# A hybrid encoder layer whose expert weights stream through a ring: the ring's slabs, the order of the loads and their size are changed

## The chip, the cores and the metric

The kernel runs on one core of one Trainium2 chip. The metric is the device time of one execution in microseconds (us). Before the change it is 1153.33 us, the median of three runs (1152.59 to 1154.02).

## The reference

One layer of an encoder over 256 tokens of width 1024: latent attention beside a convolution module, cross-attention into 256 memory tokens, and a mixture of experts; then a last RMSNorm. All in fp32. The part that matters here is the mixture (cut):

```
logits = t @ w_router + b_router              # 256 tokens, 32 experts
top_val, top_idx = lax.top_k(logits, 4)
gates = softmax(top_val)
# for the tokens of each expert e:
up = xb @ w_up[e] + b_up[e]                   # w_up[e]: 1024 x 2048, 8 MB
glu, lin = min(up[:, :1024], 7), clip(up[:, 1024:], -7, 7)
act = glu * sigmoid(1.702 * glu) * (lin + 1)
y = act @ w_down[e] + b_down[e]               # w_down[e]: 1024 x 1024, 4 MB
out = sum over the experts of a token of gate * y
return rmsnorm(x + out, g_final)
```

Each of the 32 experts has 12 MB of weights (12.58 million bytes), 402.7 million bytes in all, and every one is used once.

## The kernel before

A trunk (both mixing layers, cross-attention, router) runs first, to about 241 us. Then TensorE goes through the experts 0 to 31 in order. The tokens of an expert are taken in blocks of 64; an expert with more than 64 tokens takes a second round over the same weights (`Fori(0, extra + 1)` in `expert`), so there may be more blocks than experts. One block on PE is: the up products in four quarters (L1813), the combine of the block before (L1773), transposes of the up result (L1866), the one-hots of the combine (L1909, L1911), the gather for the next block (L1760), the first half of the down products (L1858), the columns of the next block (L1767), the second half of the down products (L1858).

**The ring.** `ring` is 20 slabs of 8 KB in each of the 128 partitions (1 MB a slab). Two slabs are a group, also called a slot: 10 slots. An expert is six groups: up 0 to 3 (the quarters of the up products) and down 4 and 5 (the halves). Here (e, i) stands for group i of expert e. Group i of expert e lies in slot (6e + i) modulo 10 (`slot_of`). During the trunk the ring holds the trunk's weights and temporaries.

**The queue of loads.** All weight loads are issued by SP, in program order, on one queue of the 16 DMA engines. Before each load SP waits until PE has finished with what lies in its slots: `up_steps` counts PE's used up quarters, `down_steps` its used down halves, and `last_block(e)` reads from a table which block is the last one of expert e. An SP wait holds back every load behind it.

- Experts 2, 3 and 28 to 31: loads of one group (2 MB, 16 KB in a row per partition), L446 and L450.
- Experts 4 to 27 (`load_expert_wide`): three loads of two groups each (4 MB, 32 KB in a row per partition). The first two, L511, bring up 0 and 1, then up 2 and 3; the third, L523, the down weights. Their waits are:

```
sp.wait_ge(up_steps, n2 * UPS + UPS)        # n2: last block of e - 2
load_wide(up_v, e, j * LOADS, 0)
sp.wait_ge(down_steps, n2 * DOWNS + DOWNS)
load_wide(up_v, e, j * LOADS, 2)
sp.wait_ge(up_steps, n1 * UPS + DOWNS)      # n1: last block of e - 1
```

PE waits for the semaphore of a load before the first group in it.

**Loops.** SP and PE have the experts 0 to 6 written out, 7 to 26 in a loop of four turns of five experts (10 slots and 6 groups repeat after five experts), and the last five written out. DVE, ACT and GpSimd loop over the experts.

**Around the first expert.** Before the table of blocks is known, SP loads expert 0 whole and the up weights of expert 1 (all 20 slabs) and `g_final` (L473, into half of `buf_v`). The down weights of expert 1 follow in four loads of one slab (L489), as PE frees the first four slabs; for that, expert 0's first two quarters are computed in halves (`first_up_half`).

**The last expert** is taken in smaller pieces, so that little is left after its last load. Its output, scaled by `g_final`, goes through `buf_x` to HBM.

## Time and profile before

| | before |
|---|---|
| median of three runs | 1153.33 us |
| the profiled execution | 1153.83 us |
| its span in the trace | 1152.1 us |
| around the span | 1.73 us |
| PE busy | 1130.9 us (98%) |
| bytes read from HBM | 436.18 MB, 379 GB/s over the span |

The profile page gives for each engine its busy time, then the span in 40 slices with the granted clock of TensorE and the rate of the DMA engines, then the chain of work that ended last. TensorE's clock was granted at full speed (1.00) in all but a few slices late in the expert stage (0.91 from 920 to 940 and from 980 to 1000 us). A busy share of PE near 1 tells little alone: it also has to be seen where PE waits for a load, and whether the DMA engines pause. "To landing" is the time from the issue of a load on SP to the semaphore that tells of its end; a load that stands in the queue behind others takes longer to land than it takes to move.

### The profile page before, as it was taken

To read this page: it belongs to the slowest core of one execution; us is meant where nothing else is said; L and a number is where in the kernel's file an instruction comes from. 1 tells how busy PE (TensorE), PEld (TensorE's weight loads), DVE (VectorE), ACT (ScalarE), POOL (GpSimd) and SP (SyncE) were. 2 spreads that over 40 slices of the span, in tenths; PEclk is the share of its full clock that TensorE was granted. 3 is DMA by queue.
4 is the path that set the end of the run, shared out by engine and by line. 5 is a ranking of instruction groups with operands and counts; after the bars stand their busy time and mean duration, and the time that the engine had idled before them with its cause. 6 is when DMAs were issued, how large, how long until landed. Compare 5 with 4: busy or idle time off the path is not lost.

```text
span 1152.1 us, 16029 instructions
## 1 busy us (share of the span) xinstructions
PE 1130.9 (98%) x5376; PEld 502.2 (44%) x5377; DVE 358.9 (31%) x933; ACT 221.7 (19%) x429; POOL 85.2 (7%) x206
## 2 busy tenths in 40 slices
PE   9999999999999999999999999999999999999999
PEld 6785487653333333333333333333333333333333
DVE  6898413232222222222222222222222222222223
ACT  5321213121111121111111111111111111111113
POOL 2990000000000000000000000000000000000000
PEclk9999999999999999999999999999999999999999
DMA  9464336389999999999999999999999999999995
GB/s 364 188 272 176 146 146 282 156 347 429 429 435 431 427 433 433 427 432 433 396 421 437 437 422 433 437 432 423 437 437 424 431 437 433 424 426 429 424 426 244
DMA packets 28821, 437.76 MB, mean 380 GB/s; under 512 B 4017, under 2 KB 4657, under 8 KB 12017
## 3 DMA queue, kind: packets, MB, share of 16 engines
q1 hardware_dynamic: 27920, 436.10, 89.4%
q10 hardware_dynamic: 864, 1.14, 0.3%
q8 instruction: 27, 0.44, 0.2%
q14 instruction: 10, 0.07, 0.0%
HBM read 436.18 MB, written 1.05 MB: 379 GB/s over the span
## 4 chain that ended last, share of the span: by engine, by line
PE 77%; DMA 20%; SPq 1%; ACT 1%; issue 0%; DVE 0%; ACTq 0%; DVEq 0%
PE bank L1813 28%; DMA ring<-in_w_up_dram 20%; PE bank L1858 16%; PE total L1773 4%; PE bank L1760 4%; PE bank L1452 2%; PE bank L1471 2%; PE bank L1866 2%; PE bank L1683 2%; PE bank L1462 2%; PE bank L1767 1%; PE bank L1617 1%; PE total L1617 1%; DMA ring<-in_w_in_dram 1%; PE bank L1911 1%; PE bank L1576 1%
## 5 line engine op out<-in xcount | busy, mean ns | idle before, releaser
L1813 PE MATMUL bank<-ring,buf_m 128*64 128x512 f32 (+1 forms) x2192 | 465.2, 581 | 13.4 <-DMA ring<-in_w_up_dram 13.3
L1813 PEld LDWEIGHTS bank<-ring,buf_m 128*64 128x64 f32 x2192 | 156.9, 138 | 316.1 <-issue 286.4
L1858 PE MATMUL bank<-ring,buf_m 128*64 128x512 f32 x1056 | 239.9, 595 | 0.0
L1343 DVE COPY buf_f<-bank 128x512 f32<-128x512 f32 x32 | 22.1, 692 | 448.6 <-PE bank L1813 448.6
L1858 PEld LDWEIGHTS bank<-ring,buf_m 128*64 128x64 f32 x1056 | 72.8, 136 | 136.5 <-issue 126.5
L888 ACT ACTIVATE buf_m<-buf_f 128x256 f32<-128x256 f32 x32 | 13.3, 416 | 333.1 <-DVE buf_f L1353 333.1
L1773 PE MATMUL total<-buf_m,wr_sb 64*128 64x512 f32 x272 | 67.6, 615 | 1.6 <-ACT buf_m L897 0.8
L656 POOL TENSOR_TENSOR buf_v<-table,buf_v 128x4 f32<-128x4 f32 x33 | 6.6, 201 | 775.6 <-DVE buf_v L1331 775.3
L1760 PE MATMUL bank<-buf_k,buf_v 128*64 128x512 f32 x264 | 63.9, 605 | 0.0
L1349 DVE TENSOR_TENSOR buf_f<-bank,buf_v 128x512 f32<-128x512 f32 x64 | 44.0, 687 | 57.7 <-PE bank L1866 57.7
L897 ACT ACTIVATE buf_m<-bank,buf_v 128x512 f32<-128x512 f32 x32 | 22.0, 687 | 194.1 <-PE bank L1858 194.1
L1304 DVE TENSOR_TENSOR buf_m<-bank,channel_vecs 128x256 f32<-128x256 f32 x68 | 25.7, 420 | 84.0 <-PE bank L1767 82.9
L884 ACT ACT_TABLE_LOAD x32 | 41.1, 1283 | 33.0 <-issue 33.0
L1076 DVE SCALAR_TENSOR_TENSOR ring<-ring,channel_vecs 128x256 f32<-128x256 f32 x90 | 46.7, 566 | 1.1
L1773 PEld LDWEIGHTS total<-buf_m,wr_sb 64*128 64x128 f32 x272 | 23.4, 186 | 44.9 <-issue 41.6
L886 ACT ACTIVATE buf_f<-bank 128x512 f32<-128x512 f32 x32 | 19.1, 597 | 117.3 <-PE bank L1813 117.3
L1866 PEld LDWEIGHTS bank<-ident,buf_f 128*128 128x128 f32 x256 | 27.4, 141 | 24.3 <-issue 24.3
L1866 PE MATMUL bank<-ident,buf_f 128*128 128x128 f32 x256 | 35.0, 280 | 0.0
L631 POOL TENSOR_SCALAR buf_f<-ring,channel_vecs 128x256 f32<-128x256 f32 x30 | 32.3, 1076 | 0.0
L1357 DVE SCALAR_TENSOR_TENSOR buf_f<-buf_f 128x256 f32<-128x256 f32 x64 | 27.2, 425 | 6.7
L1452 PE MATMUL bank<-buf_v,ring 128*128 128x256 f32 x128 | 28.3, 379 | 0.0
L1471 PE MATMUL bank<-ring,buf_m 128*128 128x512 f32 x64 | 28.1, 592 | 0.0
(389 smaller groups left out, 884.4 us busy)
## 6 DMA issues: line engine op xcount, KB each, us to landing
ring<-in_w_up_dram SPq DMA_DIRECT2D x48, 4096.0 KB, 30.0
ring<-in_w_down_dram SPq DMA_DIRECT2D x24, 4096.0 KB, 30.4
ring<-in_w_up_dram SPq DMA_DIRECT2D x29, 2048.0 KB, 15.3
ring<-in_w_down_dram SPq DMA_DIRECT2D x13, 2048.0 KB, 38.2
ring<-in_w_down_dram SPq DMA_DIRECT2D x6, 1024.0 KB, 10.8
ring<-in_w_up_dram SPq DMA_DIRECT2D x6, 1024.0 KB, 38.5
ring<-in_w_in_dram SPq DMA_DIRECT2D x4, 1024.0 KB, 17.2
ring<-in_w_xkv_dram SPq DMA_DIRECT2D x2, 2048.0 KB, 27.4
```

Of the source, the lines that this page charges most:

```text
L631: g.tensor_scalar(prod, src, wt, None, ALU.mult).then_inc(conv_prod_ready, 1)
L884: a.activation(scrap[:, 3:4], eps[:, 0:1], ACT.Sigmoid)
L1076: ins = v.scalar_tensor_tensor(acc[:, c, :], src, wt, acc[:, c, :], ALU.mult, ALU.add)
L1349: v.tensor_tensor(A_sb[:, js], banks[2 + i].rearrange("p (j h t) -> p j h t", j=4, h=2), bias, ALU.add).then_inc(biased, 1)
L1357: v.scalar_tensor_tensor(lin, lin, 1.0, glu, ALU.add, ALU.mult).then_inc(prod_ready, 1)
L1452: ins = t_.matmul(b[:, g * T:(g + 1) * T], wc_sb[:, c, k, g * P:(g + 1) * P], hTn[:, k, :], start=k == 0 and g == 0, stop=k == KT - 1 and ...
L1471: ins = t_.matmul(b[:, :], mT[:, k, a * P:(a + 1) * P], wv_sb[:, k, n * BANK:(n + 1) * BANK], start=k == 0, stop=k == KT - 1)
L1760: ins = t_.matmul(banks[bank][h * 64:(h + 1) * 64, :], P2v[:, a, h * 64:(h + 1) * 64], by_half[:, a, h], start=a == 0, stop=a == 1)
L1773: ins = t_.matmul(banks[4 + 2 * a + h], PT2[h * 64:(h + 1) * 64, a * P:(a + 1) * P], y_sb[h * 64:(h + 1) * 64, :], start=False, stop=last)
L1813: ins = t_.matmul(banks[bank][h * 64:(h + 1) * 64, c0:c1], xg[:, k, :], w[:, :, k % 4, h, :], start=first, stop=last)
L1858: ins = t_.matmul(banks[2][h * 64:(h + 1) * 64, :], actT[:, f, :], group(slot_of(at))[:, lo + h * BANK:lo + (h + 1) * BANK], start=f == 0, ...
L1866: ins = t_.transpose(banks[2 + c][:, f % 4 * P:(f % 4 + 1) * P], U_sb[:, f * P:(f + 1) * P], ident[:, :])
```

## The change

- The ring has 22 slabs (11 slots). The two new ones are the buffers `buf_x` (slab 20) and `buf_m` (slab 21), which the trunk uses; what `buf_m` held in the expert stage goes into `buf_v`, `U_sb` and `A_sb`, and `gates2` into `wr_sb`.
- `homes()` gives every group its slot: modulo 11 up to expert 13; from expert 14 on, slot 0 is left out, so 10 slots remain. Slot 0 then takes `g_final` and the output.
- `transfers(e)` gives the loads of an expert. Experts 14 to 25 bring all four up groups in one load of 8 MB (64 KB in a row per partition) where their slots lie in a row: that is 14, 15, 17 to 20 and 22 to 25. The other experts from 4 to 27 keep pairs, and 5, 9 and 12 have a pair split in two where it would cross the ring's end.
- `wait_free` waits for what lay in the last slot of a load before.
- All experts are written out on SP and PE.
- `g_final` is loaded last; expert 1's down weights come in two loads of two slabs, the first of them into slabs 20 and 21 as soon as PE has used the residual.
- Expert 0's first half is no longer computed in halves; PE starts each block on `xg_half` and waits for `xg_ready` a quarter later.

The core of the diff:

```diff
-RING, LOADS, CYCLE = 20 // GROUP, 12 // GROUP, 5
-TURNS = (E - 2) // CYCLE - 1
+RING, LOADS = 22 // GROUP, 12 // GROUP
+SHORT_FROM = 14
...
+def homes():
+    first = [q % RING for q in range(SHORT_FROM * LOADS)]
+    after = first[-1] + 1
+    short = [slot for slot in list(range(after, RING)) + list(range(after)) if slot]
+    return first + [short[q % len(short)] for q in range((E - SHORT_FROM) * LOADS)]
+HOME = homes()
...
+def group_before(e, i):
+    q = e * LOADS + i
+    return divmod(max(p for p in range(q) if HOME[p] == HOME[q]), LOADS)
...
+def transfers(e):
+    at = HOME[e * LOADS:(e + 1) * LOADS]
+    if not WIDE_FROM <= e < WIDE_TO:
+        return [(i,) for i in range(LOADS)]
+    if SHORT_FROM <= e < WIDE_TO - 2 and at[:UPS] == list(range(at[0], at[0] + UPS)):
+        return [tuple(range(UPS)), tuple(range(UPS, LOADS))]
+    pairs = [(i, i + 1) for i in range(0, LOADS, 2)]
+    return [p for i, j in pairs for p in ([(i, j)] if at[j] == at[i] + 1 else [(i,), (j,)])]
...
-        ring = sb("ring", 20 * SLAB)
+        ring = sb("ring", 22 * SLAB)
...
-        buf_x = sb("buf_x", TT * D)
+        buf_x = slab(20)
-        buf_m = sb("buf_m", KT * T)
+        buf_m = slab(21)
...
-        gfin = buf_v[:, 0:D]
+        gfin = slab(0)[:, 0:D]
-        out_sb = buf_x[:, :].rearrange("p (a n) -> p a n", a=TT)
+        out_sb = slab(1).rearrange("p (a n) -> p a n", a=TT)
-        xg = buf_m[:, 0:512].rearrange("p (k s) -> p k s", k=KT)
-        sig = buf_m[:, 512:1024].rearrange("p (j t) -> p j t", j=KT)
-        actT = buf_m[:, 1024:1536].rearrange("p (j t) -> p j t", j=KT)
-        y_sb = buf_m[:, 1536:2048]
+        xg = buf_v[:, 0:512].rearrange("p (k s) -> p k s", k=KT)
+        sig = U_sb.rearrange("p (j s) -> p j s", j=KT)[:, :, 0:CAP]
+        actT = A_sb[:, :, 1, :]
+        y_sb = buf_v[:, 512:1024]
...
+            def wait_free(e, i, n1, n2):
+                e_before, i_before = group_before(e, i)
+                n = n1 if e_before == e - 1 else n2
+                if i_before < UPS:
+                    sp.wait_ge(up_steps, n * UPS + (i_before + 1))
+                else:
+                    sp.wait_ge(down_steps, n * DOWNS + (i_before - UPS + 1))
+            def load_expert(e):
+                n2, n1 = last_block(e - 2), last_block(e - 1)
+                for piece in transfers(e):
+                    i = piece[0]
+                    wait_free(e, piece[-1], n1, n2)
+                    ...
+                        load(e, i, len(piece))
...
-            with sp.Fori(1, TURNS) as turn:
-                for j in range(2, 2 + CYCLE):
-                    load_expert_wide(turn * CYCLE + j, j)
...
+            for e in range(2, E - 1):
+                load_expert(e)
+            load_last_expert()
...
+                    pe.wait_ge(xg_half, n + 1)
+                    up_group(e, 0, range(4))
+                    pe.wait_ge(xg_ready, n + 1)
+                    up_group(e, 1, range(4, KT))
```

What stands on SP around the first expert, before the change (L446: up 2 and 3 of expert 0; L473: `g_final`; L489: one slab of expert 1's down weights; L479, L480: reads of the table):

```order
L446 DMA ring<-in_w_up_dram 128x4096 x2
L473 DMA buf_v<-in_g_final_dram 128x1024
L479 TENSOR_LOAD meta_i [waits psum_drained_by_vector]
L479 ISA x2
L480 TENSOR_LOAD meta_i
L480 ISA x2
L492 ISA
L489 DMA ring<-in_w_down_dram 128x2048 [waits first_quarter_slabs_of_first_expert_used]
```

And with the change (L488: the same up groups; L492: one group of expert 1's down weights; L522, L523: reads of the table):

```order
L488 DMA ring<-in_w_up_dram 128x4096 x2
L492 DMA ring<-in_w_down_dram 128x4096 [waits expert_rows_ready,last_residual_in_total]
L522 TENSOR_LOAD meta_i [waits psum_drained_by_vector]
L522 ISA x2
L523 TENSOR_LOAD meta_i
L523 ISA x2
L528 ISA
L492 DMA ring<-in_w_down_dram 128x4096 [waits up_slabs_used]
```

The load of `g_final` is gone from here, and a group of expert 1's down weights stands ahead of the read of the table.

The loads of one wide expert on SP before the change, here expert 4; the loop repeats the same waits and loads for expert 14 (L516, L518, L521: registers for the waits):

```order
L516 ISA
L511 DMA ring<-in_w_up_dram 128x8192 [waits up_slabs_used]
L518 ISA
L511 DMA ring<-in_w_up_dram 128x8192 [waits down_slabs_used]
L479 TENSOR_LOAD meta_i
L479 ISA x2
L480 TENSOR_LOAD meta_i
L480 ISA x2
L521 ISA
L523 DMA ring<-in_w_down_dram 128x8192 [waits up_slabs_used]
```

With the change, expert 14 (L535: every load from expert 2 on; L548, L550: registers for the waits):

```order
L522 TENSOR_LOAD meta_i
L522 ISA x2
L523 TENSOR_LOAD meta_i
L523 ISA x2
L550 ISA
L535 DMA ring<-in_w_up_dram 128x16384 [waits down_slabs_used]
L548 ISA
L535 DMA ring<-in_w_down_dram 128x8192 [waits up_slabs_used]
```

Two up loads with a wait each have become one, with the later kind of wait only: the load that waited for up quarters is gone. The one wait is for the group that lay in the last of the four slots: for expert 14 that is (12, 4), for expert 15 (13, 5).

## Rows read from the trace of the kernel before

**Rows 1.** The page: GB/s in each of 40 equal slices of the span.
```profile
GB/s 364 188 272 176 146 146 282 156 347 429 429 435 431 427 433 433 427 432 433 396 421 437 437 422 433 437 432 423 437 437 424 431 437 433 424 426 429 424 426 244
```

**Rows 2.** Window 568 to 576; last three: granted clock, DMA share, GB/s.
```profile
568.00:576.00 8.00, 8.00 (x40) 2.64 (x38) 0.00 (x0) 0.60 (x1) 0.00 (x0) 1.00 0.79 307
```

**Rows 3.** Waits of PE on loads, and of SP on PE: us, times, longest.
```profile
PE bank L1813 <- DMA ring<-in_w_up_dram: 13.3, 10, 2.2
...
543.17 7.09 PE L1813 MATMUL bank<-ring,buf_m 128*64 128x512 f32 x32 [1.14 <-DMA ring<-in_w_up_dram]
...
SPq L523 <- PE bank L1813: 148.5, 24, 33.1
```

**Rows 4.** The chain of waits, PE: start us, us, engine and line.
```profile
589.94 13.73 PE bank L1813 x64
...
609.05 3.43 PE bank L1858 x16
613.07 3.58 PE bank L1858 x16
```

**Rows 5.** SP in order of time: start us, us, line of the issue.
```profile
522.40 13.28 SPq L511 DMA_DIRECT2D ring<-in_w_up_dram  x2
570.29 0.33 SPq L523 DMA_DIRECT2D ring<-in_w_down_dram  x1
...
623.70 0.33 SPq L523 DMA_DIRECT2D ring<-in_w_down_dram  x1
630.59 13.28 SPq L511 DMA_DIRECT2D ring<-in_w_up_dram  x2
650.41 0.33 SPq L523 DMA_DIRECT2D ring<-in_w_down_dram  x1
```

**Rows 6.** Issues at 535.35, 623.70, 650.41 us; last number: us to landing.
```profile
ring<-in_w_up_dram SPq DMA_DIRECT2D x1, 4096.0 KB, 36.9
ring<-in_w_down_dram SPq DMA_DIRECT2D x1, 4096.0 KB, 18.5
ring<-in_w_down_dram SPq DMA_DIRECT2D x1, 4096.0 KB, 21.0
```

**Rows 7.** Line 523: ns min/median/max, first and last start; landing.
```profile
L523 SPq DMA_DIRECT2D ring<-in_w_down_dram x24: 327/333/342, 328.4 to 980.1; - x24
...
DMA to landing us min/median/max: 12.4/30.4/41.2
```

**Rows 8.** Line 446: the same.
```profile
L446 SPq DMA_DIRECT2D ring<-in_w_up_dram x29: 327/328/3024, 177.4 to 1074.1; - x29
...
DMA to landing us min/median/max: 7.1/15.3/45.3
```

**Rows 9.** g_final, issued at 235.01 us; last number: us to landing.
```profile
buf_v<-in_g_final_dram SPq DMA_DIRECT2D x1, 512.0 KB, 13.1
```

**Rows 10.** Line 489, the four slabs after it.
```profile
L489 SPq DMA_DIRECT2D ring<-in_w_down_dram x4: 327/328/332, 243.1 to 248.3; - x4
...
DMA to landing us min/median/max: 7.5/10.0/11.1
```

**Rows 11.** DMA queues from 240 to 600 us: packets, MB, share.
```profile
q8 instruction: 13, 0.21, 0.2%
```

**Rows 12.** DMA queues from 600 to 960 us, the only queue listed.
```profile
q1 hardware_dynamic: 5344, 155.72, 100.5%
```

**Rows 13.** SP issues expert 8's up weights, and us to landing.
```profile
415.57 13.32 SPq L511 DMA_DIRECT2D ring<-in_w_up_dram  x2
ring<-in_w_up_dram SPq DMA_DIRECT2D x1, 4096.0 KB, 28.9
ring<-in_w_up_dram SPq DMA_DIRECT2D x1, 4096.0 KB, 27.2
```

**Rows 14.** PE's last wait for a load; DVE's first use of g_final.
```profile
1134.23 1.59 PEld L1813 LDWEIGHTS bank<-ring,buf_m 128*64 128x64 f32 x16 [0.56 <-DMA ring<-in_w_up_dram]
1144.28 1.23 DVE L1390 TENSOR_TENSOR buf_x<-total,buf_v 128x1024 f32<-128x1024 f32 x1 [5.18 <-ACT buf_x L929]
```

More of the change, by code:

```diff
@@ L40, with arrivals @@
 BANK = 512
+def homes():
[15 more added lines that the diff above has]
+    return [p for i, j in pairs for p in ([(i, j)] if at[j] == at[i] + 1 else [(i,), (j,)])]
+def arrivals():
+    found, counts = {}, [0] * RING
+    for e in range(E):
+        for piece in transfers(e):
+            slot = HOME[e * LOADS + piece[0]]
+            counts[slot] += 1
+            for p in piece:
+                found[e, p] = (slot, counts[slot])
+    return found
+ARRIVAL = arrivals()
 def trunk_jobs():
@@ L472, in _ @@
             load_up(0, 0, 3)
[L473 removed]
+            sp.wait_ge(residual_kept, 1)
+            sp.wait_ge(rows_ready, TT)
+            load_down(1, LOADS, 0)
             wait_drained(sp, "meta")
@@ L571, in _, with load @@
-            sp.wait_ge(up_steps, n1 * UPS + 2)
-            for q in range(2):
-                load_slab(down_v, E - 1, at, UPS + 1, 1, q, last_down_in[q])
+            sp.wait_ge(up_steps, n1 * UPS + 1)
+            load_down(1, LOADS, 1)
+            def load(e, i, n=1):
+                slot = slot_of(e * LOADS + i)
+                w, lo = (up_v, i) if i < UPS else (down_v, i - UPS)
+                sp.dma_start(slab(slot * GROUP, n * GROUP), w[e, :, lo * WIDE:(lo + n) * WIDE]).then_inc(group_in[slot], 16)
@@ new lines, in load_expert, with load_last_expert @@
+            def load_expert(e):
+                n2, n1 = last_block(e - 2), last_block(e - 1)
+                for piece in transfers(e):
+                    i = piece[0]
+                    wait_free(e, piece[-1], n1, n2)
+                    if e == E - 2 and i == UPS - 1:
+                        load_slab(e, i, 0, late_up_in)
+                        load_slab(e, i, 1, group_in[slot_of(e * LOADS + i)])
+                    else:
+                        load(e, i, len(piece))
+            def load_last_expert():
+                n2, n1 = last_block(E - 3), last_block(E - 2)
+                for i in range(2):
+                    wait_free(E - 1, i, n1, n2)
+                    load(E - 1, i)
+                wait_free(E - 1, 3, n1, n2)
+                for k in range(2):
+                    load_slab(E - 1, 2 + k, 0, last_up_in[0][k])
+                wait_free(E - 1, 4, n1, n2)
+                load(E - 1, 4)
+                for k in range(2):
+                    load_slab(E - 1, 2 + k, 1, last_up_in[1][k])
+                wait_free(E - 1, 5, n1, n2)
+                for q in range(2):
+                    load_slab(E - 1, 5, q, last_down_in[q])
+                sp.wait_ge(up_steps, n1 * UPS + 2)
+                sp.dma_start(gfin, g_final.rearrange("(a n) -> a n", a=1).broadcast_to([P, D])).then_inc(loaded["late"], 16)
@@ L1799, in _, with wait_loaded @@
             pe.wait_ge(loaded["bdown"], 32)
-            def wait_loaded(turn, at):
-                uses = turn * (CYCLE * LOADS // RING) + (at // RING + 1)
-                if slot_of(at) % 2:
-                    alone = [q for q in range(E * LOADS) if slot_of(q) == slot_of(at)
-                             and not WIDE_FROM <= q // LOADS < WIDE_TO]
-                    uses = 1 + alone.index(turn * CYCLE * LOADS + at)
-                pe.wait_ge(group_in[slot_of(at)], uses * 16)
+            def wait_loaded(e, i):
+                slot, count = ARRIVAL[e, i]
+                pe.wait_ge(group_in[slot], count * 16)
             def up_products(w, bank, c0, c1, k, first, last):
@@ L1878, in down_group, with expert @@
                 ins.then_inc(down_steps, 1)
-            def expert(e, turn, j, rounds=None, wide=False, late=False):
+            def expert(e, rounds=None):
                 extra, first = rounds or rounds_of(e)
```

161 lines of the change are left out of this document (36 added, 125 removed).

## The prediction

> **What bounds the kernel now.** I read the slices of the page first, then the waits, then the single loads. From slice 9 (about 230 us) to the last but one the DMA engines move 420 to 437 GB/s, with one dip to 396 [rows 1]. So in the expert stage the DMA queue is nearly always full, and the 402.7 million bytes of expert weights set the time. PE needs 26.71 us for a block (589.94 to 613.07 + 3.58) [rows 4]. The loads need more: expert 14's down weights land at 623.70 + 18.5 = 642.2 us [rows 5, 6], expert 27's at 980.1 + 41.2 = 1021.3 [rows 7]. That is 13 experts, 163.6 million bytes, in 379.1 us: 431.5 GB/s, 29.16 us an expert, 9.72 us a load of 4 MB. PE starts ahead with a full ring, loses 2.45 us of lead an expert, and waits when the lead is gone; its waits on loads are 13.3 us in all [rows 3], nearly all late. At the end it still waits for a load, at 1134.23 us [rows 14]. So a microsecond on the load queue is a microsecond on the kernel, as long as the queue doesn't run empty.
>
> It runs empty once. Expert 11 has two rounds: SP waits 33.1 us, the longest of these waits, for the first quarters of its last round [rows 3], and the load of expert 12's down weights goes out only at 570.29 [rows 5]. The load before it, issued at 522.40 + 13.28 - 0.33 = 535.35, lands at 572.25 [rows 6]. From 568 to 576 us the engines move 307 GB/s [rows 2]. By landings: seven loads, 68.05 us of work, take from 572.25 to 642.2, so the pause costs 1.9 us.
>
> **The change part by part.** The sum is made against the profiled execution, 1153.83 us (span 1152.1 and 1.73 around it), 0.5 above the median of the three runs; I carry its differences over to the median.
>
> *The opening.* `g_final` lands at 235.01 + 13.1 = 248.1 [rows 9]; its 0.52 million bytes are 1.2 us of the queue, and now go last. There they are hidden: DVE first uses `g_final` at 1144.28 [rows 14], five us after PE had the last weights. The four slabs behind it land by 248.3 + 11.1 = 259.4 [rows 10], 11.3 us for 9.8 us of bytes: 1.5 us of gaps. With the change the first two of these slabs wait only for the residual (about 241 us), so the queue doesn't run dry. The queue is then 1.2 + 1.5 = 2.7 us ahead. The group `(11, 2..3)`, for which PE waits 1.14 us at 543 [rows 3], comes in time, and PE is 1.14 us earlier from there on.
>
> *Twenty-two slabs and the second round of expert 11.* The load that lands at 572.25 now lands at 569.55. Behind it stand (12, 4) and (12, 5), then three loads of expert 13. Their waits end in time. (12, 5) needs (11, 0) of the second round, one quarter (3.43) before 570.29 and 1.14 earlier: 565.7. The loads of 13 need (11, 2), (11, 4) and (12, 0): about 572.6, 584.7 and 592.3, each more than 3 us before the queue ends. So the old pause is gone. The loads land at 579.4 for expert 12, and at 579.4 + 3 x 9.72 = 608.5 for expert 13.
>
> *The first load of eight slabs.* Expert 14's up weights go to slots 7 to 10, which held (12, 1) to (12, 4). The one load waits for (12, 4), the first half of expert 12's down products. PE ends it at 609.05 + 3.43 - 1.14 = 611.3 [rows 4]; SP issues at 611.4. But the queue is empty from 608.5. A load into a nearly empty queue takes 12.4 us to land, the shortest of line 523 [rows 7], 2.7 more than its 9.7 us of bytes. So this one lands at 611.4 + 2.7 + 19.4 = 633.5 instead of 627.9: a pause of 5.6 us. Expert 14's down weights follow at 643.2.
>
> *The second.* Expert 15's up weights go to slots 3 to 6, the last of them (13, 5), used at the end of block 13. Before, SP's same wait ended at 643.54 (630.59 + 13.28 - 0.33) [rows 5]; less 1.14 that is 642.4. The load lands at 642.4 + 2.7 + 19.4 = 664.5, unpaused it would be 662.6: 1.9 us. Expert 15 is complete at 674.2, where before it was at 650.41 + 21.0 = 671.4 [rows 5, 6]. So at this point the queue is **2.8 us behind**, whatever it had won before: both restarts are timed by PE. From here no wait bites: expert 17's up load needs the end of block 15, 642.2 + 2 x 26.7 = 695.6, and the queue lasts to 674.2 + 29.2 = 703.4; later the margin grows by 2.45 us an expert. What is late next is PE: it gets to expert 17 at 722.3, its up weights land at 722.8, and from there it waits in nearly each expert. Since it needs all four groups before it starts, it stands 6.9 us (two quarters) later in the cycle than with pairs; the narrower loads from expert 26 on let it catch up by expert 30.
>
> *Longer runs.* Loads of 16 KB runs: from 1021.3 to 1074.1 + 45.3 = 1119.4 [rows 8], 41.9 million bytes in 98.1 us, 427.5 GB/s. Runs of 32 KB give 431.5, 0.93% more. If that is a cost per packet, doubling again gives half as much, 0.46%; eight such loads after expert 15 are 155 us, so 0.7 us. Bounds: nothing, or 0.93% again (1.4). I take 0.7.
>
> *Code written out.* From 240 to 600 us, where SP's and PE's code is mostly straight, there are 13 instruction packets [rows 11]; from 600 to 960, inside the loop, none [rows 12]. With the change they go on to the end. What they cost: the landings of expert 8's first two loads are 444.5 (415.57 + 28.9) and 455.8 (428.56 + 27.2) [rows 13], 11.3 us apart instead of 9.7. That is the one irregular gap I found in 240 to 560 us, and the packets may be its cause. The loop's 360 us would get as many: 0 to 1.6 us, and I take 0.8. The Trainium skill ("Runtime: NRT & Kernel Launch", Instruction fetch mechanics) says that code is refilled in 16 KiB blocks and that a taken branch forces a fetch before execution goes on, which makes it prefer full unrolling. By that rule the loop would be the slower form; rows 12 show no fetch in it at all.
>
> *The rest at nothing.* PE's own work is the same products; expert 0's first half costs PE the same passes in another order. The zeroing of `gates2` now waits for the second logits, 2 us later, about 3 us before DVE needs it. If the new places of `actT` and `sig` made a block slower, 15 blocks (to block 13, expert 11 twice) would stand on the path: 0.05 us each would be 0.75 us.
>
> **Sum:** 2.8 - 0.7 + 0.8 = 2.9 us: 1156.7 for the profiled execution, about **1156.2 us** on the median (+0.25%).
>
> **Rivals.**
>
> *The larger ring pays (not slower).* If the load for expert 14 is issued by 605.8 us (608.5 less 2.7), the queue never runs empty. Then the 2.7 of the opening, the 1.9 of the old pause and the 0.7 of the longer runs are all kept: 1153.3 - 5.3 = 1148.0. For it: two slabs more are 4.9 us of work for the queue just when expert 11 repeats. Against it: the wait is for (12, 4), and PE would have to be there 5.6 us earlier. As pairs, the first load could go at about 599 and there would be no pause; as one load it can't. 0.10.
>
> *The gains nearly cancel the pause (no change).* Longer runs at 1.4, no cost of the code, the same pause: 2.8 - 1.4 = 1.4, 1154.7. For it: I found only one irregular gap for 13 packets. Against it: the rate of a longer run has no row here. 0.20.
>
> *Instruction packets hurt (clearly slower).* If each of some 16 packets in 600 to 1020 us held up the engine that ends last by about half a microsecond, that would be 8 us: 1164. Two irregular gaps like that of expert 8 give 2.8 - 0.7 + 3.2 = 5.3, 1158.6, and I weigh the rival there. Against the larger figure: from expert 8's second load (455.8) to expert 12's (572.25) it is 29.1 us an expert, with the same packets beside them, no more than in the loop. 0.11.
>
> *A fixed price per load that merging saves.* With 2.7 us per load, eight loads fewer would bring 21.6 us: 1131.7. But then the 4.19 million bytes of a load would move in 9.72 - 2.7 us, 597 GB/s, and no slice has over 437 [rows 1]. 0.01. The Trainium skill ("DMA: Bandwidth & Descriptors", Anatomy of one DMA) gives about 2.0 us fixed and bytes at 436 GB/s; that fits a load into an empty queue here (2.7), not one in a full queue (0).
>
> **How the numbers follow.** The forecast's mechanism has 0.58; its own range is 1155 to 1158.5 (terms at their bounds: 2.8 - 1.4 to 2.8 + 1.6 and something for blocks). A measurement of this kernel tells about 0.2% from no change, 1151.0 to 1155.6. Of the forecast's 0.58 some 0.13 lie below 1155.6. Slower: 0.45 + 0.11 and a little of the second rival: 0.57. Same: 0.13 + most of 0.20: 0.32. Faster: 0.11. The range for 8 in 10 is 1151.5 to 1160.5: it leaves out the larger ring's full gain and the packets at their worst.
>
> **What would show it.** Right: no dip at 568 to 576 us; a DMA dip of about 5 us between 607 and 614, and one of 2 us near 643; expert 15 complete about 3 us later than before; PE's regular waits from about 722 us instead of 865, in sum some 3 us longer; expert 11's wait of 1.14 us gone; instruction packets between 600 and 960. Wrong: an issue of expert 14's up load before 606 us, a queue that never dips, or loads of 8 MB that land 19.1 us apart or less.

## The result: 7.7 to 8.3 us slower, where 2.9 were forecast

| | before | after |
|---|---|---|
| median, first comparison | 1153.58 us | 1161.9 us (1160.6 to 1163.1) |
| ratio, 95% interval | | 1.007 (1.0057 to 1.0082) |
| the profiled execution | 1153.83 | 1162.86 |
| its span | 1152.1 | 1161.1 |

The direction was right, the size was not: 1161.9 lies above the range of 1151.5 to 1160.5.

The queue of loads comes first. The page of the changed kernel, GB/s in 40 equal slices, answers [rows 1]. Under it a table of windows answers [rows 2]; its last three numbers are granted clock, DMA share and GB/s:

```profile
GB/s 353 195 250 194 144 146 271 163 351 427 433 433 431 430 427 428 433 432 432 431 412 367 396 433 433 433 432 433 433 434 432 431 433 430 430 426 425 428 425 224
```

```profile
568.00:576.00 8.00, 8.00 (x40) 2.73 (x38) 0.00 (x0) 0.60 (x1) 0.00 (x0) 1.00 0.96 412
...
608.00:616.00 8.00, 8.00 (x40) 2.73 (x42) 3.86 (x12) 1.65 (x5) 0.00 (x0) 1.00 0.52 193
636.00:644.00 8.00, 8.00 (x42) 2.77 (x40) 3.43 (x12) 1.24 (x4) 0.24 (x2) 1.00 0.91 393
```

The old pause at 569 is gone; two new ones stand near 611 and 643, where they were forecast. SyncE's issues there, and for the issues at 613.28, 644.16 and 651.03 the time from issue to landing (last number), against [rows 5, 6]:

```profile
613.28 0.33 SPq L535 DMA_DIRECT2D ring<-in_w_up_dram  x1
624.32 0.33 SPq L535 DMA_DIRECT2D ring<-in_w_down_dram  x1
644.16 0.33 SPq L535 DMA_DIRECT2D ring<-in_w_up_dram  x1
651.03 0.33 SPq L535 DMA_DIRECT2D ring<-in_w_down_dram  x1
...
ring<-in_w_up_dram SPq DMA_DIRECT2D x1, 23.1
ring<-in_w_up_dram SPq DMA_DIRECT2D x1, 24.3
ring<-in_w_down_dram SPq DMA_DIRECT2D x1, 4096.0 KB, 27.1
```

Expert 15 is complete at 651.03 + 27.1 = 678.1 us, forecast 674.2. TensorE's waits on loads, and its first regular one, against [rows 3]:

```profile
PE bank L1822 <- DMA ring<-in_w_up_dram: 16.4, 9, 6.1
...
726.86 15.65 PE L1822 MATMUL bank<-ring,buf_v 128*64 128x512 f32 x64 [2.62 <-DMA ring<-in_w_up_dram]
```

The DMA queues from 600 to 960 us, against [rows 12] (q1 carries the weights; q8 and q14 carry instructions, q8 those of TensorE, as the run on TensorE alone shows below):

```profile
q8 instruction: 14, 0.23, 0.2%
q14 instruction: 2, 0.02, 0.0%
```

### The profile page after: what moved, and what is told of

It is laid out like the page before. It is cut to its first block, busy times and chain, and to the rows that moved or that the text cites. A ratio compares the mean times of both kernels' runs of the same rounds, so it can differ in the third digit from the quotient of the medians.

```text
span 1161.1 us, 15769 instructions
## 1 busy us (share of the span) xinstructions
PE 1134.0 (98%) x5344; PEld 507.3 (44%) x5344; DVE 358.9 (31%) x933; ACT 221.6 (19%) x429; POOL 85.0 (7%) x206
## 3 DMA queue, kind: packets, MB, share of 16 engines
q10 hardware_dynamic: 864, 1.14, 0.3%
## 4 chain that ended last, share of the span: by engine, by line
PE 80%; DMA 19%; ACT 1%; issue 0%; SPq 0%; DVE 0%; ACTq 0%; DVEq 0%
PE bank L1822 31%; DMA ring<-in_w_up_dram 18%; PE bank L1856 16%; PE total L1786 4%; PE bank L1773 4%; PE bank L1465 2%; PE bank L1484 2%; PE bank L1864 2%; PE bank L1696 2%; PE bank L1475 2%; PE bank L1780 1%; PE bank L1630 1%; PE total L1630 1%; DMA ring<-in_w_in_dram 1%; PE bank L1904 1%; PE bank L1589 1%
## 5 line engine op out<-in xcount | busy, mean ns | idle before, releaser
L1822 PE MATMUL bank<-ring,buf_v 128*64 128x512 f32 (+1 forms) x2160 | 467.6, 590 | 16.5 <-DMA ring<-in_w_up_dram 16.4
L1822 PEld LDWEIGHTS bank<-ring,buf_v 128*64 128x64 f32 x2160 | 162.6, 138 | 317.3 <-issue 308.6
L1856 PE MATMUL bank<-ring,buf_f 128*64 128x512 f32 x1056 | 239.9, 595 | 0.0
L1356 DVE COPY buf_f<-bank 128x512 f32<-128x512 f32 x32 | 22.1, 692 | 455.5 <-PE bank L1822 455.5
L1856 PEld LDWEIGHTS bank<-ring,buf_f 128*64 128x64 f32 x1056 | 72.8, 136 | 136.5 <-issue 124.9
L901 ACT ACTIVATE buf_f<-buf_f 128x256 f32<-128x256 f32 x32 | 13.3, 416 | 316.8 <-DVE buf_f L1366 316.8
L1786 PE MATMUL total<-buf_v,wr_sb 64*128 64x512 f32 x272 | 67.6, 615 | 1.6 <-ACT buf_v L910 0.8
L910 ACT ACTIVATE buf_v<-bank,buf_v 128x512 f32<-128x512 f32 x32 | 22.0, 687 | 194.2 <-PE bank L1856 194.2
L1317 DVE TENSOR_TENSOR buf_v<-bank,channel_vecs 128x256 f32<-128x256 f32 x68 | 25.7, 420 | 84.0 <-PE bank L1780 82.9
L1786 PEld LDWEIGHTS total<-buf_v,wr_sb 64*128 64x128 f32 x272 | 23.4, 186 | 44.9 <-issue 41.6
L1864 PEld LDWEIGHTS bank<-ident,buf_f 128*128 128x128 f32 x256 | 27.4, 140 | 24.3 <-issue 24.3
L1465 PE MATMUL bank<-buf_v,ring 128*128 128x256 f32 x128 | 28.3, 379 | 0.0
L1484 PE MATMUL bank<-ring 128*128 128x512 f32 x64 | 28.1, 592 | 0.0
```

Source lines behind the costliest of these rows:

```text
L1465: ins = t_.matmul(b[:, g * T:(g + 1) * T], wc_sb[:, c, k, g * P:(g + 1) * P], hTn[:, k, :], start=k == 0 and g == 0, stop=k == KT - 1 and ...
L1484: ins = t_.matmul(b[:, :], mT[:, k, a * P:(a + 1) * P], wv_sb[:, k, n * BANK:(n + 1) * BANK], start=k == 0, stop=k == KT - 1)
L1786: ins = t_.matmul(banks[4 + 2 * a + h], PT2[h * 64:(h + 1) * 64, a * P:(a + 1) * P], y_sb[h * 64:(h + 1) * 64, :], start=False, stop=last)
L1822: ins = t_.matmul(banks[bank][h * 64:(h + 1) * 64, c0:c1], xg[:, k, :], w[:, :, k % 4, h, :], start=first, stop=last)
L1856: ins = t_.matmul(banks[2][h * 64:(h + 1) * 64, :], actT[:, f, :], group(slot_of(at))[:, lo + h * BANK:lo + (h + 1) * BANK], start=f == 0, ...
L1864: ins = t_.transpose(banks[2 + c][:, f % 4 * P:(f % 4 + 1) * P], U_sb[:, f * P:(f + 1) * P], ident[:, :])
```

## How the runs are read

Two things are read from each profile beside its time. One is the **start**: when TensorE's first product of expert 0 begins, here in the changed kernel (before: 241.14 us).

```profile
243.30 7.09 PE L1822 MATMUL bank<-ring,buf_v 128*64 128x512 f32 x32
```

The other is the list of **late landings**: loads that land more after the one before them than their bytes take in a full queue (9.7 us for 4 MB, 4.9 for 2 MB, 19.4 for 8 MB). This table is worked out from the profiles. Packets are those of q8 between 590 and 1000 us; late landings stand with their excess in us (to about 0.1), between 440 and 1090 us. The kernels are explained with the experiments:

```
kernel                    start   packets  late landings (excess)
before                   241.14     0      455.8 (1.6)  restart: 582.7 (0.7)  603.4 (1.2)
before, again            241.46     0      455.9 (1.5)                        1012.0 (1.5)
before, loop written out 242.23    16      456.4 (1.3)  604.1 (1.8)  800.0 (1.6)  1015.2 (1.6)
 the same, again         243.67    16      457.9 (1.5)  605.6 (1.6)  801.5 (1.7)  1016.6 (1.5)
 on TensorE alone        242.17    16      456.2 (1.3)  604.3 (1.8)  800.3 (1.5)  1015.4 (1.4)
 half of it              241.63    11      454.9 (1.2)  729.5 (1.5)  944.6 (1.5)
after                    243.30    16      465.9 (1.5)  636.4 (5.2)  668.5 (2.9)  844.6 (1.6)  1045.1 (1.6)
 again                   242.75    16      464.8 (1.4)  635.9 (5.7)  667.2 (2.1)  843.2 (1.5)  1043.8 (1.6)
 again                   242.58    16      464.9 (1.4)  635.7 (5.4)  667.7 (2.9)  843.8 (1.5)  1049.2 (1.6)
after, pairs             242.60    16      464.5 (1.4)  679.9 (1.5)  875.7 (1.5)  1086.7 (1.6)
after, long from 17      242.03    16      464.3 (1.5)  679.6 (1.5)  729.2 (0.9)  934.2 (0.8)
after, loop of 5         241.46    11      463.1 (1.3)  634.3 (5.8)  665.4 (1.9)  1006.3 (1.0)
pairs, loop of 5         241.42    11      462.7 (1.3)  678.0 (1.3)  1019.5 (1.3)
pairs, loop of 11        241.20    18      462.7 (1.2)  678.2 (1.4)  835.1 (1.2)  1031.1 (1.1)
before, g_final last     241.96     0      456.1 (1.4)  restart: 585.1 (2.7)
pairs, 3 turns from 15   242.01     9      464.0 (1.3)  679.4 (1.3)
pairs, 3 turns from 14   241.62     8      463.4 (1.3)  restart: 630.0 (1.2)  728.7 (1.1)
```

A third number tells where a loss lies. From the landing of the last weights to the end of the span it is 13.0 us in sixteen of the seventeen profiles, and 15.1 in "3 turns from 15". So in the sixteen the time changes only with the start and with the time that the queue takes from there to the last weights.

## The experiments

**The changed kernel again.** No edit; a second time for its profile alone.

> The changed kernel once more, nothing edited. Theory: of the 8.3 us it is slower, some 5 to 6 belong to the pauses before the two first 8-slab loads (experts 14 and 15) and some 3 to irregular gaps of 11 us in place of 9.6 between landings after 600 us. If these gaps come from instruction packets they stand at about the same places again (landings near 844 and 1045), and the pauses at 607 to 614 and near 643 stand there again whatever the gaps do. The late start (expert 0's first product at 243.3 in place of 241.2) came with one issue of 3.1 us at the very beginning: if it is chance, the start is 241.2 to 243.4 here and the time 1160.8 to 1163.0; if it belongs to the change, the start is 243.3 again. Time 1161 to 1163.

> The changed kernel a third time, for its start: 243.30 and 242.75 us so far. Chance: anywhere from 241.2 to 243.3. The program's: 242.7 to 243.3. Time 1160.8 to 1163.1, and late landings at the same two loads as before (landed 844.6 and 1045.1).

1161.45 us (1160.8 to 1162.8; ratio to before 1.007, 1.0056 to 1.0084), and 1162.04. Both pauses and the late landings up to 844 us stand at the same loads three times, and the last one at the same load twice and one load later the third time (1049.2). So they belong to the program. The start was 242.75 and 242.58.

**The loop written out in the kernel before.** On SyncE and TensorE:

```
-with sp.Fori(1, TURNS) as turn:      # and the same on pe
+for turn in range(1, TURNS):
     for j in range(2, 2 + CYCLE):
```

> The kernel before with one edit: the loop over experts 7 to 26 on SyncE and TensorE is written out; ring, loads and waits stay. Theory (written-out code costs): instruction packets appear on the queues every 25 us between 600 and 1000 as in the changed kernel, and two or three landings come 1.5 us late because of them; with the queue full all of that reaches the end: 1153.6 + 2 to 4 = 1155.5 to 1157.5. Rival (the packets are hidden, or the late landings of the changed kernel came from something else): 1153.6, within 0.5.

1158.01 us, ratio 1.0037 (1.0023 to 1.0051): 4.3 us for the form of the code alone, over half of the whole loss and above what I expected of this run. The prediction had 0.8 for it.

**On TensorE alone.** The same edit, only in TensorE's code.

> The kernel before with the loop over experts 7 to 26 written out on TensorE alone; SyncE keeps its loop. Theory (it is TensorE's instructions that fill the DMA queue's instruction packets): packets of q8 every 25 us, none of q14 between 600 and 1000, and nearly all of the 4.3 us of the kernel with both written out: 1156.5 to 1158. Rival (it is SyncE that loses, because it stops for its own code while loads should be issued): no or few of the 4.3 us, 1153.7 to 1155.

1157.99 us, 1.0038 (1.0024 to 1.0052). The whole loss comes with TensorE's code, and q14 has no packet from 600 to 960 us. The issues around one late landing, their landings (28.3, 31.2, then 35.5 us after the issue), and the packets from 600 to 960 us:

```profile
751.05 0.33 SPq L511 DMA_DIRECT2D ring<-in_w_up_dram  x1
757.92 0.33 SPq L523 DMA_DIRECT2D ring<-in_w_down_dram  x1
764.80 13.28 SPq L511 DMA_DIRECT2D ring<-in_w_up_dram  x2
...
ring<-in_w_up_dram SPq DMA_DIRECT2D x1, 4096.0 KB, 28.3
ring<-in_w_down_dram SPq DMA_DIRECT2D x1, 4096.0 KB, 31.2
ring<-in_w_up_dram SPq DMA_DIRECT2D x1, 4096.0 KB, 35.5
```

```profile
q1 hardware_dynamic: 5318, 154.86, 100.0%
q8 instruction: 14, 0.23, 0.3%
```

757.92 + 31.2 = 789.1 and 764.80 + 35.5 = 800.3: 11.2 us apart for 9.7 us of bytes, in a queue at 100%. In the trace's records each of these packets takes its DMA engine for 1.0 to 1.1 us, and in the twelve that I followed (596 to 872 us) a packet of weights that starts as it ends takes 1.67 to 1.76 us in place of 1.21. Together that is 1.5 to 1.6 us on one engine. From the fourth packet behind the pause at 570 on, their durations come back in the same order every eight packets (1.02, 1.02, 1.07, 1.07, 1.06, 1.11, 1.10, 1.09 us).

The landings show which engines are hit. The semaphore of each load gets sixteen increments in the trace, and the load has landed with the last of them. I read them as one for each of the 16 engines; the records don't name the engine. Worked out from this run, behind the pause at 570 us:

```
load landed  packets since the pause   increments up to 0.5 us before the last   the others, us before it
583.1        0                         16
604.3        1                          1                                        1.3 to 1.8
623.7        2                          2                                        1.3 to 1.8
653.1        3                          3                                        1.5 to 2.0
682.3        4                          4                                        1.5 to 2.0
701.7        5                          5                                        1.6 to 2.0
730.8        6                          6                                        1.6 to 2.0
760.0        7                          7                                        1.6 to 2.0
789.1        8                          8                                        1.6 to 2.0
800.3        9                          1                                        1.5 to 3.5
```

Each packet puts one more engine 1.5 us back, until eight are back; the eight others are not hit in this stretch. The ninth packet comes to an engine that is back already, and only then does a load land late again. So the round goes over eight of the 16 engines, and of eight packets in a row one is seen in the landings, with 1.5 us: here the 1st (604.3), the 9th (800.3) and the 17th (1015.4) after the pause at 570 had levelled the engines. The other runs agree: of the 21 steps from one late landing to the next with no pause between them, 19 have eight packets in them; the other two have nine and seven, in the loop of eleven, where three packets crowd into 12 us. What fixes the round isn't shown.

**Half of the loop written out.** TensorE's turns for experts 17 to 26.

```
-with pe.Fori(1, TURNS) as turn:
+with pe.Fori(1, 3) as turn:          # experts 7 to 16; then 17 to 26:
+for turn in range(3, TURNS):
```

> The kernel before with half of TensorE's loop written out: experts 7 to 16 in the loop, 17 to 26 written out; SyncE as it was. Theory (a step of about 1.5 us for each 8 packets of written-out code): 8 or 9 packets of q8 between 730 and 1000 us, one late landing there, and half of the 4.3 us: 1155.3 to 1156.3. Rival (a lump: the start, or leaving the loop at all): 1157.5 to 1158, or 1153.8 and nothing.

1157.05 us, 1.0026 (1.0016 to 1.0036): 3.3 us, neither half nor all. The late landings say why. From 560 to 720 us only q1 moves data; from 718 to 730 there is the first packet of q8, and the load issued at 703.35 is late:

```profile
696.48 0.33 SPq L511 DMA_DIRECT2D ring<-in_w_up_dram  x1
703.35 0.33 SPq L523 DMA_DIRECT2D ring<-in_w_down_dram  x1
...
ring<-in_w_up_dram SPq DMA_DIRECT2D x1, 4096.0 KB, 21.8
ring<-in_w_down_dram SPq DMA_DIRECT2D x1, 4096.0 KB, 26.1
```

```profile
q1 hardware_dynamic: 174, 5.18, 100.4%
q8 instruction: 1, 0.02, 0.6%
```

696.48 + 21.8 = 718.3, 703.35 + 26.1 = 729.5: 11.2. The next seven packets (750 to 908 us) leave no mark, and the ninth (933 us) makes the load of 944.6 late. Two steps of 1.5 in place of one are what the count of packets gives: my expectation of half the loss missed because I had forgotten that the first packet behind a pause costs in full.

**No loads of eight slabs.** Two lines of `transfers` go:

```
-    if SHORT_FROM <= e < WIDE_TO - 2 and at[:UPS] == list(range(at[0], at[0] + UPS)):
-        return [tuple(range(UPS)), tuple(range(UPS, LOADS))]
```

> The changed kernel with one edit: no transfer of eight slabs, all of experts 4 to 27 load in transfers of four slabs; ring 22 then 20, code written out, g_final last as in the changed kernel. Theory (the pauses before the first 8-slab loads cost the time): no pause at 607 to 614 nor at 643, the queue is full from 250 to the end, and the time falls by what the pauses cost and more, since the pause at 569 and the wait of 1.14 of the kernel before are gone as well: 1162 - 5.2 - 2.9 (the two landings 24.6 and 22.3 apart in place of 19.4) + 0.7 (the longer runs' gain lost) = 1154.6, and 1.6 to 3 less where the last expert-by-expert restarts of the 8-slab loads also cost: 1151.5 to 1155. Rival (the smaller ring from expert 14 is what makes the queue run empty, whatever the size of the loads): a pause stays near 607 and the time is 1159 or more.

1155.15 us, 1.0012 (1.0003 to 1.0021): the loads of eight slabs, with their pauses, cost 6.3 us. The same windows in this kernel; it never pauses:

```profile
568.00:576.00 8.00, 8.00 (x40) 2.59 (x36) 0.00 (x0) 0.60 (x1) 0.00 (x0) 1.00 1.00 426
606.00:614.00 8.00, 8.00 (x47) 3.58 (x47) 4.74 (x12) 1.65 (x5) 0.00 (x0) 1.00 0.99 426
640.00:648.00 8.00, 8.00 (x40) 2.61 (x38) 1.88 (x8) 2.17 (x3) 0.60 (x3) 1.00 1.00 422
```

**Eight slabs only from expert 17.**

```
-    if SHORT_FROM <= e < WIDE_TO - 2 and ...
+    if 17 <= e < WIDE_TO - 2 and ...
```

> The changed kernel with one edit: transfers of eight slabs only from expert 17 (in place of 14), experts 14 to 16 in transfers of four. Theory (an 8-slab load caps how far the loads run ahead of TensorE, and the pause comes wherever the first of them comes while the lead is larger): no pause at 607, one pause at about 693 of about 4 us (the waits of expert 17's first load end with expert 15's last product), and the time lies between the other two: 1162 - 8 + 4 + 0.7 = about 1158 to 1159. Rival (the pause at 607 belongs to the step from 22 to 20 slabs at expert 14, not to the size of the load): the pause stays at 607 and none is at 693, time 1161 to 1163.

1156.38 us, 1.0023 (1.0014 to 1.0032), only 1.2 over pairs. The place of the pause was as expected, the price was not. There is no dip at 607 and one at 693, of (1 - 0.81) x 8 = 1.5 us in the mean of the engines:

```profile
606.00:614.00 8.00, 8.00 (x43) 3.25 (x43) 4.45 (x12) 1.65 (x5) 0.00 (x0) 1.00 0.99 426
692.00:700.00 8.00, 8.00 (x42) 2.96 (x42) 2.01 (x8) 2.17 (x3) 0.60 (x3) 1.00 0.81 309
```

```profile
696.30 0.33 SPq L535 DMA_DIRECT2D ring<-in_w_up_dram  x1
...
ring<-in_w_up_dram SPq DMA_DIRECT2D x1, 22.3
```

The load before it lands at 699.1, 2.8 us behind the issue, and this one at 718.6, 19.5 later: the landings show no pause at all. The packets had put the slowest engine about 1.5 us behind the others (679.6), and it was the others that idled. It also says that the merged loads bring little: eight of them land 19.35 to 19.64 us behind the load before, two pairs take 19.43, and the kernel is slower than pairs. In a full queue, in the changed kernel, a merged load takes 19.35: 0.08 less than two pairs, some 0.6 us for eight.

**g_final last, in the kernel before.** The load of L473 goes behind the last weights, DVE's wait to its product with `g_final`.

> The kernel before with one edit: g_final's row is loaded after the last weights instead of before the first expert, and VectorE waits for it only at the final product. Theory (the load holds up the weights behind it, and the lead is 1.2 us short until TensorE's wait of 1.14 us in expert 11): that wait is gone or nearly, all that TensorE frees later comes 1.1 us earlier, the pause at 569 ends 1.1 earlier, and the time is 1153.6 - 1.1 = 1152.5. Rival (the lead is lost again at the pause near 569, or paid back at the end where g_final now lands last): no change, 1153.6, within 0.4.

1154.34 us against 1153.94, 1.0005 (0.9996 to 1.0014): no gain. TensorE's wait in expert 11 was 0.70 in place of 1.14, so at most 0.4 was to be had there, in place of the 1.1 that I had expected. In this profile the restart at 570 took 14.4 us from issue to landing in place of 12.4, with fifteen of the sixteen increments at 12.1 us or before. But the profiled execution, 1156.39 us, is the slowest of the eleven, 2 us above the median, so this restart doesn't explain the median. Why it came is open.

**The changed kernel with a loop.** Experts 15 to 24 as two turns of five, on SyncE and TensorE (10 slots and six groups repeat after five experts here too):

```
+with sp.Fori(0, 2) as turn:
+    for e in range(15, 20):
+        load_expert(e, turn * 5 + e)      # the waits, slots and sizes of e
...                                           # and the same on pe
```

> The changed kernel, transfers of eight slabs and all, with one edit: experts 15 to 24 as a loop on SyncE and TensorE (two turns of five experts). Theory (the pauses and the instruction packets add up: behind a pause all 16 DMA engines start level, so that the next packet delays the next load in full): the first 8-slab load keeps its 23 us from issue to landing or nearly, the second one falls from 23.6 to 24.3 to about 22.5, the late landing near 843 is gone, and the time is 1161.5 - 2.5 to 4 = 1157.5 to 1159. Rival (an 8-slab load with 64 KB runs has a restart of its own that is 1 to 2 us dearer): the second load keeps its 23.6 or more, and the time falls by 1.5 at most, to 1160.

1159.06 us, 1.0047 (1.0034 to 1.0061): 2.4 less. The landing near 843 is in time. The load of expert 15 lands 22.9 us behind its issue in place of 23.6 to 24.3, between the two theories; it still has packets beside it, since the first turn of the loop is fetched too.

**The same with pairs.** Both edits together.

> The changed kernel with all loads of experts 4 to 27 in transfers of four slabs (as in e2_after_pairs), and in addition experts 15 to 24 as a loop on SyncE and TensorE (two turns of five experts); experts 0 to 14 and 25 to 31 stay written out. Theory (each instruction packet holds up one of the 16 DMA engines by 1.1 to 1.6 us, and a load lands when the engine that was hit most often is done): no instruction packets between about 670 and 920, one or two of the three late landings after 600 us are gone (each 1.5), and the time is 1155.15 - 1.5 to 3.0 = 1152.2 to 1153.7. Rival (the late landings have another cause, and the 4.3 us of the written-out kernel came from TensorE or SyncE themselves): late landings stay, 1155.1.

1152.64 us (1151.7 to 1153.8, 11 runs), before beside it 1153.94: 0.9992 (0.9983 to 1.0001). It is 2.5 below pairs written out, and has the lowest median of the study, but it isn't shown to beat the kernel before. From 700 to 910 us:

```profile
q1 hardware_dynamic: 3110, 90.57, 100.3%
q8 instruction: 4, 0.07, 0.1%
```

**A loop of eleven experts.** 22 slabs up to expert 25, experts 4 to 25 as two turns of eleven, pairs.

> As e7_pairs_loop5, but the ring stays at 22 slabs up to expert 25, and the loop is two turns of eleven experts (4 to 14, 15 to 25), since 22 slabs and twelve slabs an expert repeat after eleven experts. Theory A (the body of eleven experts is fetched again in each turn, as written-out code is): instruction packets every 25 us all along, time as with pairs alone, 1155 within 1. Theory B (a loop body of this length stays where TensorE finds it, as that of five experts in the kernel before does): packets only in its first turn or not at all, late landings after 600 us gone, 1155.15 - 3 to 4.5 = 1150.7 to 1152.2.

1154.61 us, 1.0006 (0.9997 to 1.0015). Packets every 25 us all along, 18 in place of 16, as theory A had it: a body of eleven experts is fetched again in each turn, one of five isn't. Straight code has 16 packets in 410 us, 1.1 an expert, so that by my estimate the two bodies are some 6 and some 12 packets of 16 KB. Where between them the limit lies isn't measured.

**Three turns.** First experts 15 to 29 in the loop, with loads of four slabs up to 29; then experts 14 to 28, with four slabs up to 28.

> As e7_pairs_loop5, with three turns of the loop (experts 15 to 29) and transfers of four slabs up to expert 29 (before: 27); experts 0 to 14, 30 and 31 written out. Theory (every 200 us of written-out code the DMA engine that was hit most often gets one instruction packet more, 1.1 to 1.6 us): no packets from 690 to 1070 us, one late landing less than with two turns: 1152.64 - 1 to 1.6 = 1151.0 to 1151.6; wider loads of experts 28 and 29 give or take nothing at the end, since the last load alone sets it. Rival (the loop gives nothing in the middle, and what e7_pairs_loop5 won against pairs alone lay at its start by chance): 1152.6 or more.

> As e7_pairs_loop5, with 22 slabs up to expert 12, the loop over experts 14 to 28 (three turns of five) and transfers of four slabs up to expert 28; experts 0 to 13 and 29 to 31 written out. Theory (packets cost by their number, and e10_pairs_loop5x3 lost its gain because wide loads of expert 29 left TensorE behind at the end): packets as few as in e10_pairs_loop5x3, last weights landed about 4 us earlier than in e7_pairs_loop5 as seen from the start, TensorE no more behind them than there: 1152.6 - 1.5 to 4 = 1148.6 to 1151.1. Rival (the wide loads are not what kept TensorE behind; three turns give nothing over two): 1152.6 to 1154.

1153.99 us (0.9998, 0.9989 to 1.0007) and 1153.19 (0.9994, 0.9985 to 1.0003): both miss their forecast. From the start to the last weights the queue takes 896.0 us with two turns (241.42 to 1137.4), 894.9 with three from expert 15 (242.01 to 1136.9) and 896.2 with three from expert 14 (241.62 to 1137.8).

In the first the queue gains 1.1 us, as the one late landing less (1019.5) lets expect. But TensorE ends 15.1 us behind its last weights, in all other profiles 13.0: with wide loads for expert 29 it starts its last three experts later than its work allows. The second keeps narrow loads there and is back at 13.0, with 8 packets to 11. It loses the gain elsewhere. The ring has 22 slabs up to expert 13 in it too, but in the first turn of the loop the loads wait as in the later turns, where the ring is shorter. SyncE issues the second up load of expert 14 at 602.96 + 13.30 - 0.34 = 615.9 us, and with two turns at 599.17 + 12.56 - 0.33 = 611.4. First two turns, then three from expert 14, with the time of its second load from issue to landing:

```profile
599.17 12.56 SPq L555 DMA_DIRECT2D ring<-in_w_up_dram  x2
...
602.96 13.30 SPq L555 DMA_DIRECT2D ring<-in_w_up_dram  x2
...
ring<-in_w_up_dram SPq DMA_DIRECT2D x1, 4096.0 KB, 14.1
```

The load lands at 630.0, 10.9 us behind the one before: a new pause of 1.2 us. So both loops of three turns have fewer packets, and each pays for it at another place.

**Two more looks at the start.**

> The kernel before once more, for its start alone. In its one profile so far TensorE's first product of expert 0 started at 241.14 us; in seven profiles of kernels with the changed trunk it was 241.20 to 243.30. Theory (the start varies from run to run, by which load of the opening is issued late): 241 to 243 here. Rival (it belongs to the program): 241.1 within 0.2. Time 1153 to 1154.5.

> The kernel before with the whole loop written out on both engines, once more, for its start. If the written-out code delays the start by about 1 us, TensorE's first product of expert 0 starts at 242.0 to 242.5 again; if that was chance, it may be 241.2. Time 1157.4 to 1158.1 or, by chance, 1 us less.

241.46 (1154.28 us) and 243.67 (1158.90 us). Over all profiles, eight with all experts written out on TensorE start at 242.03 to 243.67 (mean 242.7), nine with a loop at 241.14 to 242.01 (mean 241.5). The means differ by 1.1 us, but the groups all but touch (242.03 and 242.01), and two profiles of the same program are up to 1.4 apart (242.23 and 243.67, the second outside what I expected of it). By what way the code of the experts could reach a part that is over before them isn't shown.

## Why the prediction was wrong

The direction was right, and so was its main reason: two pauses that cost more than the opening wins. The size was wrong. In three parts, by medians. Written-out code: 4.3. The larger ring, the opening and `g_final` (pairs less the written-out kernel before, 1155.15 - 1158.01): -2.9. The loads of eight slabs (1161.45 - 1155.15): 6.3. The sum is 7.7, and so much it was beside these runs; the first comparison had 8.3. Of the 4.8 us that the forecast lacked, about 3.5 are the first part and 1.7 the second; the third gave 0.5 back.

- **Code written out: 0.8 forecast, 4.3 measured.** This step failed. It found one late landing beside 13 packets and took half of its 1.6 us, as if one such landing might or might not come in the loop's 360 us. It was the first sign of a rule: one step of 1.5 us for each round of eight packets, and one at once behind each pause. The written-out kernels have three such steps behind 600 us; the kernel before has one late landing there in each of its two profiles (1.2 and 1.5). From the start to the last weights they take 900.3, 900.4 and 900.8 us, the kernel before 898.0 and 898.1: 2.2 to 2.8 us. The later start is about 1 more, and the rest of the 4.3 is within what the executions of one kernel differ by. The prediction's rival had the mechanism, "the engine that ends last", and for two gaps like that of expert 8 the price of 3.2 us; it got a chance of 0.11, because the 29.1 us an expert between 455.8 and 572.25 seemed to speak against any cost. Only four packets lie there, and by the rule of eight no step was due.
- **Opening and old pause: 2.7 + 1.9 = 4.6 forecast, 2.9 measured.** Both terms were too large. Up to the load ahead of the old pause (expert 12's up 2 and 3) pairs take 328.95 us from the start (571.55 - 242.60) and the written-out kernel before 330.80 (573.03 - 242.23): 1.85 of the 2.7. The 1.9 of the pause were read from one profile: 0.8 at the restart and 1.2 at the load that landed at 603.4. That was a second restart, which the prediction's "it runs empty once" passes over: the load was issued 2.3 us ahead of the landing before it. A second profile of the same kernel has both restarts, with landings 12.2 and 11.9 us after the issue, and the load of 623.83 lands 17.2 after its own:

```profile
570.42 0.33 SPq L523 DMA_DIRECT2D ring<-in_w_down_dram  x1
577.30 13.32 SPq L511 DMA_DIRECT2D ring<-in_w_up_dram  x2
...
623.83 0.33 SPq L523 DMA_DIRECT2D ring<-in_w_down_dram  x1
...
ring<-in_w_down_dram SPq DMA_DIRECT2D x1, 4096.0 KB, 12.2
ring<-in_w_up_dram SPq DMA_DIRECT2D x1, 4096.0 KB, 11.9
ring<-in_w_down_dram SPq DMA_DIRECT2D x1, 4096.0 KB, 17.2
```

  There the same seven loads take 572.4 to 641.1, 0.6 us over their 68.05. In the first profile one increment of sixteen was 1.2 late at 603.4, with no instruction packet in sight; why is open. The pause is cheap because it is timed by the issue: in the six profiles of the kernel before and its written-out forms the new load lands 12.1 to 12.4 us behind it, whatever the slowest engine had lost before. So the pause swallows the 1.5 of the late landing at 456. Taking the pause away took this cover away too. That the text didn't see: its sentence that "a microsecond on the load queue is a microsecond on the kernel" holds for the slowest engine, not for the mean.
- **The two pauses: 5.6 + 1.9, less 0.7 for longer runs, 6.8 forecast, 6.3 measured.** Right in place, and in size partly by luck. By landings the pauses are 5.2 to 5.7 and 2.1 to 2.9, together 7.8 to 8.3 and more than the 7.5 forecast; but they also swallow a late landing that pairs have (679.9, 1.5 us). The restart's 2.7 was too small: 23.1 and 24.3 us from issue to landing are 3.7 and 4.9 more than 19.4, with one packet beside each, which behind a pause costs in full.
- **Longer runs: 0.7 forecast, about 0.6 by landings in a full queue.** Right, and too small to show in the time: no kernel with them is faster than pairs.
- **Signs.** Right: no dip at 569, dips near 611 and 643, the wait of 1.14 gone, regular waits from 724 us, 3.1 us more of them in sum (16.4 against 13.3), instruction packets from 600 to 960. Off: expert 15 is complete at 678.1, 6.7 us later than before, not 2.8. Of the 3.9 more, 1.8 are the later issue of its first load (644.16, not 642.4) and 2.2 the landing (24.3 us, not 22.1). That issue stands 400.9 us behind the start in all three profiles of the changed kernel, so it came late with the start. The steps at 844 and 1045 came on top.

The Trainium skill ("Runtime: NRT & Kernel Launch", Instruction fetch mechanics) prefers full unrolling, because a taken branch to code outside the two pages at hand forces a fetch. In this case the measurement decides against it: a body of five experts, some six packets of 16 KB, runs with no fetch in the trace [rows 12], and writing it out costs 0.37%.

The fixed 2.0 us that the prediction takes from the Trainium skill ("DMA: Bandwidth & Descriptors", Anatomy of one DMA) are given there for transfers that GpSimd issues. The loads here are issued by SyncE; their restart at the old pause shows 2.4 to 2.7 us beyond the 9.7 of 4 MB.

## What to carry to other kernels

Where one DMA queue is the bound and full, count everything that uses a DMA engine beside it, the instructions of the busiest engine too, and price it on the slowest of the 16 engines, not on their mean. A price read from one profile may be half chance, as the old pause was: take a second profile before building on it. A merged load waits for the last slot it covers: ask not what it saves per transfer (here 0.08 us), but how much lead it gives away and whether the queue then runs dry. And before a pause is taken away, ask what it hid.

## What the runs showed of the hardware

- Instruction packets of TensorE's code come every 25 us of straight code, 16 KB each, hold one DMA engine for 1.0 to 1.1 us and the packet of weights behind them for 0.5 more. They go round over eight of the 16 engines, and show in the landings as mostly 1.2 to 1.6 us once every eight packets, some 200 us; the first one behind a pause shows at once.
- A loop body of five experts (an estimated six such packets) is fetched once, one of eleven is fetched in every turn.
- A load of 4 MB into a queue that has run dry landed 12.1 to 12.4 us behind its issue in six profiles and 14.4 in a seventh; in a full queue it lands 9.7 behind the load before it.
- An idle stretch of the queue can cost nothing: 1.5 us of mean idle time at 693 us, and the landings 19.5 apart as in a full queue.
